# Stick-breaking attention: sums over later key blocks formed on GpSimd ahead of the products with ones

## The reference

```python
z = einsum('bhqd,bhkd->bhqk', q_b, k) * scale
log_beta = log_sigmoid(z)
log_1m = where(strict, log_sigmoid(-z), 0.0)              # strict: key < query
acc = cumsum(log_1m, axis=3, reverse=True) - log_1m       # over the later keys
w = where(strict, exp(log_beta + acc), 0.0)
out = einsum('bhqk,bhkd->bhqd', w, v)
```

## Time and profile before

| | |
|---|---|
| median of the runs | 1338.36 us (1338.24 to 1340.0, 3 runs) |
| the profiled execution | span 1338.4 us, next to nothing around it |
| TensorE products | busy 1297.8 us, 97% of the span |
| TensorE weight loads | 1092.2 us, 82% (beside the products) |
| VectorE | 734.4 us, 55% |
| ScalarE | 554.5 us, 41% |
| GpSimd | 260.2 us, 19% |
| granted clock of TensorE | mean 0.990 of full |

### The profile page before, as it was taken

How to read it: one execution, slowest core, us unless ns; L and a number is a source line. 1 busy time by engine, 2 the same in 40 slices (tenths; PEclk the granted TensorE clock), 3 DMA queues, 4 the chain that set the end, 5 groups by cost and what they waited for, 6 DMA issues and landing times.

```text
span 1338.4 us, 17696 instructions
## 1 busy us (share of the span) xinstructions
PE 1297.8 (97%) x6599; PEld 1092.2 (82%) x6599; DVE 734.4 (55%) x998; ACT 554.5 (41%) x885; POOL 260.2 (19%) x205
## 2 busy tenths in 40 slices
PE   6979999999999999999999999999999999999997
PEld 5667788898888888888898888887988888887885
DVE  4777655538645445422288788686575544553223
ACT  4466666546322332222364555464453222322112
POOL 0532200025211111000051111321431111110002
PEclk8999999999999999999999999999999999999999
DMA  4412222122333333333222111311223333332331
GB/s 158 128 49 64 72 72 71 48 79 80 110 97 101 101 94 92 89 98 94 84 75 68 48 48 55 87 48 48 80 86 104 94 94 98 100 115 79 95 95 63
DMA packets 190503, 112.34 MB, mean 84 GB/s; under 512 B 13696, under 2 KB 184773, under 8 KB 190446
## 3 DMA queue, kind: packets, MB, share of 16 engines
q1 hardware_dynamic: 188636, 106.81, 27.5%
q0 software_dynamic: 640, 2.10, 0.6%
q10 hardware_dynamic: 1170, 2.66, 0.5%
HBM read 109.43 MB, written 4.74 MB: 85 GB/s over the span
## 4 chain that ended last, share of the span: by engine, by line
PE 85%; DVE 8%; ACT 3%; issue 2%; POOL 1%; DMA 0%; POOLq 0%; ACTq 0%; SPq 0%; DVEq 0%
PE banks L432 26%; PE banks L434 25%; PE banks L433 25%; PE banks L1711 3%; DVE w_lo L427 1%; PE banks L1741 1%; PE banks L1629 1%; PE banks L1458 1%; DVE logits L1420 1%; PE banks L481 1%; DVE tf L701 1%; ACT logits L1431 1%; DVE probsT_lo L1470 1%; POOL stick_lo L1728 0%; DVE u_lo L711 0%
## 5 line engine op out<-in xcount | busy, mean ns | idle before, releaser
L427 DVE TENSOR_TENSOR w_lo<-w_raw,w_hi 128x1024 fp32r<-128x1024 f32 (+3 forms) x200 | 288.2, 1444 | 270.7 <-ACT w_hi L420 270.4
L432 PE MATMUL banks<-u_hi,w_hi 128*128 128x512 f32 (+1 forms) x1112 | 425.5, 383 | 5.8 <-DVE w_lo L427 4.3
L434 PE MATMUL banks<-u_hi,w_lo 128*128 128x512 f32 (+1 forms) x1112 | 419.5, 377 | 0.0
L433 PE MATMUL banks<-u_lo,w_hi 128*128 128x512 f32 (+1 forms) x1112 | 419.2, 377 | 0.0
L420 ACT ACTIVATE w_hi<-w_raw 128x1024 fp32r<-128x1024 f32 (+3 forms) x200 | 206.1, 1031 | 282.6 <-PE banks L434 282.5
L432 PEld LDWEIGHTS banks<-u_hi,w_hi 128*128 128x128 f32 x1112 | 210.6, 189 | 45.8 <-issue 4.9
L434 PEld LDWEIGHTS banks<-u_hi,w_lo 128*128 128x128 f32 x1112 | 210.3, 189 | 38.9
L433 PEld LDWEIGHTS banks<-u_lo,w_hi 128*128 128x128 f32 x1112 | 210.5, 189 | 38.0 <-issue 1.0
L904 POOL TENSOR_TENSOR up<-up,gate 128x512 f32<-128x512 f32 x44 | 71.9, 1635 | 375.1 <-DVE up L930 358.3
L885 ACT ACTIVATE gate<-gate 128x512 f32<-128x512 f32 x44 | 27.8, 632 | 202.2 <-DVE gate L926 202.2
L1728 POOL TENSOR_TENSOR stick_lo<-softplus,stick_hi 128x1280 fp32r<-128x1280 f32 x14 | 44.1, 3162 | 157.0 <-DVE stick_hi L1724 157.0
(11 more groups left out here) (256 smaller groups left out, 1983.1 us busy)
## 6 DMA issues: line engine op xcount, KB each, us to landing
w_raw<-in_ffn_w_gate_up_dram SPq DMA_DIRECT2D x88, 512.0 KB, 3.7
w_raw<-in_ffn_w_down_dram SPq DMA_DIRECT2D x30, 512.0 KB, 3.6
w_raw<-in_sb_w_qkv_dram SPq DMA_DIRECT2D x24, 512.0 KB, 3.8
w_raw<-in_ab_w_in_dram SPq DMA_DIRECT2D x17, 512.0 KB, 3.7
w_raw<-in_ffn_w_down_dram SPq DMA_DIRECT2D x16, 448.0 KB, 3.6
w_raw<-in_ab_w_out_dram SPq DMA_DIRECT2D x8, 512.0 KB, 3.9
w_raw<-in_sb_w_out_dram SPq DMA_DIRECT2D x8, 512.0 KB, 4.7
bias_by_distance<-bias_rows ACTq DMA_DIRECT2D x1, 2560.0 KB
```

The costliest lines, as they stand in the source:

```text
L427: dve.tensor_tensor(wl[:, c.slot, 0:w], raw[:, c.slot, 0:w], wh[:, c.slot, 0:w].bitcast(F32), ALU.subtract).then_inc(w_lo, 1)
L432: nc.tensor.matmul(o, lh, rh, start=start, stop=False, skip_group_check=True)
L433: nc.tensor.matmul(o, lh, rl, start=False, stop=False, skip_group_check=True)
L434: return nc.tensor.matmul(o, ll, rh, start=False, stop=stop, skip_group_check=True)
```

## The change

In `c_pe` the three blocks of later keys that block 0 has, and the two that block 1 has, are no longer multiplied one by one. Their softplus is added up first: `later` holds, in 384 columns, the sum of blocks 1, 2 and 3 and, in 256 columns (from `LATER0`), the sum of blocks 2 and 3, each where its queries have them. Per head:

- ScalarE copies two pieces of 128 columns (`later_act`);
- GpSimd adds 128 columns, and then 384 (`later_pool`);
- ScalarE rounds all 640 columns to the hi part (`later_hi`), GpSimd subtracts for the lo part (`later_lo`); both go into `stick_hi` and `stick_lo`, which are free at that time;
- TensorE does the four triangle blocks and the one product with ones of block 2 as before, then waits for `ls_lo`, then multiplies the two sums with ones: 14 products instead of 20.

The steps are put into the written-out orders; on GpSimd both heads' steps stand ahead of `stick_lo`. The buffer `later` (640 columns) makes the stage's space larger by 96 columns a partition, and `tri_f` moves into the place of `sq_sum`.

```diff
+LATER0, LATER1, LATER = T - P, T - 2 * P, 2 * T - 3 * P
...
+            later = sb(s, "later_keys", [P, LATER])
-
-        sb(ctx, "stage_buffers", [P, 27680])
+        sb(ctx, "stage_buffers", [P, 27776])
...
-        tri_f = sb(ctx, "tri_f", [P, P])
...
+        with ExitStack() as s:
+            tri_f = sb(s, "tri_f", [P, P])
...
+        def later_act(act, p, e):
+            hh = p * 2 + e
+            act.wait_ge(ns_f, hh + 1)
+            if not (isinstance(p, int) and p == 0 and e == 0):
+                act.wait_ge(ls_lo, hh)
+            act.activation(later[:, 0:P], lsp[:, e, COL_AT[1]:COL_AT[1] + P], ACT.Copy)
+            act.activation(later[:, LATER0:LATER0 + P], lsp[:, e, COL_AT[2]:COL_AT[2] + P], ACT.Copy)\
+                .then_inc(ls_copied, 1)
+
+        def later_pool(pool, p, e):
+            hh = p * 2 + e
+            pool.wait_ge(ns_f, hh + 1)
+            if not (isinstance(p, int) and p == 0 and e == 0):
+                pool.wait_ge(ls_lo, hh)
+            nc.gpsimd.tensor_tensor(later[:, LATER0 + P:LATER], lsp[:, e, COL_AT[2] + P:COL_AT[2] + 2 * P],
+                                    lsp[:, e, COL_AT[3]:COL_AT[3] + P], ALU.add).then_inc(ls_one, 1)
+            pool.wait_ge(ls_copied, hh + 1)
+            pool.wait_ge(ls_one, hh + 1)
+            nc.gpsimd.tensor_tensor(later[:, P:LATER0], lsp[:, e, COL_AT[1] + P:COL_AT[1] + 3 * P],
+                                    later[:, LATER0:LATER], ALU.add).then_inc(ls_all, 1)
+
+        def later_hi(act, p, e):
+            hh = p * 2 + e
+            act.wait_ge(ls_all, hh + 1)
+            if not (isinstance(p, int) and p == 0):
+                act.wait_ge(sv_done, 2 * p - 1 + e)
+            act.activation(swh[:, e, 0:LATER], later[:, :], ACT.Copy).then_inc(ls_hi, 1)
+
+        def later_lo(eng, op, p, e):
+            eng.wait_ge(ls_hi, p * 2 + e + 1)
+            op(swl[:, e, 0:LATER], later[:, :], swh[:, e, 0:LATER].bitcast(F32), ALU.subtract).then_inc(ls_lo, 1)
+
         def c_pe(pe, p, e):
             hh = p * 2 + e
             pe.wait_ge(ns_lo, hh + 1)
-            Z = ZB[e]
+            def add(lt, at, parts, src, w):
+                for n in parts:
+                    mm = nc.tensor.matmul(ZB[e][:, at:at + w], lt[:, :], n[:, e, src:src + w],
+                                          start=False, stop=False, skip_group_check=True)
+                return mm
             for j in range(TT):
-                for jj in range(j, TT):
-                    at, w = COL_AT[j] + (jj - j) * P, T - P * jj
-                    lt = negtri if jj == j else negones
-                    for n in (nsh, nsl):
-                        mm = nc.tensor.matmul(Z[:, at:at + w], lt[:, :], n[:, e, COL_AT[jj]:COL_AT[jj] + w],
-                                              start=False, stop=False, skip_group_check=True)
-            mm.then_inc(c_done, 1)
+                add(negtri, COL_AT[j], (nsh, nsl), COL_AT[j], T - P * j)
+            add(negones, COL_AT[2] + P, (nsh, nsl), COL_AT[3], P)
+            pe.wait_ge(ls_lo, hh + 1)
+            add(negones, COL_AT[0] + P, (swh, swl), 0, T - P)
+            add(negones, COL_AT[1] + P, (swh, swl), LATER0, T - 2 * P).then_inc(c_done, 1)
...
             z_act_ln(act, p, 1)
+            if not last and not first:
+                split_hi(act, sb_chunk(p + 2, 0))
+            later_act(act, p, 0)
             if not last:
                 if not first:
-                    split_hi(act, sb_chunk(p + 2, 0))
                     sb_k_act(act, p + 1, q)
+                later_hi(act, p, 0)
                 split_hi(act, sb_chunk(p + 2, 1))
+            else:
+                later_hi(act, p, 0)
             if not (first or last):
                 sb_o_act(act, p - 1, 1, O_BANK)
+            later_act(act, p, 1)
+            later_hi(act, p, 1)
             if not last:
                 split_hi(act, sb_chunk(p + 2, 2))
             w_act(act, p, 0)
...
         def sb_pair_pool(pool, p, par, first=False, q_next=True, last=False):
+            for e in range(2):
+                later_pool(pool, p, e)
+                later_lo(pool, nc.gpsimd.tensor_tensor, p, e)
             if not last:
                 for e in range(2):
                     stick_lo(pool, nc.gpsimd.tensor_tensor, p, e)
```

More of the change, by code:

```diff
@@ L365, in bass_hybrid_two_layers @@
         ns_f, ns_hi, ns_lo = sem("softplus_ready"), sem("softplus_hi"), sem("softplus_lo")
+        ls_copied, ls_one, ls_all = sem("later_copied"), sem("later_third_added"), sem("later_second_added")
+        ls_hi, ls_lo = sem("later_hi"), sem("later_lo")
         c_done, w_exp, sw_hi, sw_lo = sem("stick_sums"), sem("stick_exp"), sem("stick_hi"), sem("stick_lo")
```

## The result

The changed kernel takes 1350.72 us (median of 4 executions, 1350.03 to 1352.82) against 1339.07 in the same comparison (1338.24 to 1340.0): ratio 1.0088, interval 1.0076 to 1.01, so 0.9% slower, 11.7 us. The forecast was 1360, slower, with a range of 1341 to 1367. Direction and range held; the size was 9 us too high. The profiled execution has a span of 1348.1 us and a granted clock of 0.987.

The account below looks back on a forecast made before the run. TensorE, never idle in the middle windows, was taken as the bound. 1338.4 + 4.8 (first pair) + 2.5 (its clock fall) + 5.4 (pairs 1 to 5) + 3.4 (their clock) + 5.2 (pairs 6, 7) = 1359.7, so 1360; range 1341 to 1367.

Parts of the forecast that it names:

- The turns of GpSimd and VectorE: Stick-breaking stage: the two engines shut each other out and alternate whole instructions, making sb_scale 2.2 us late in a middle pair.
- a middle pair: Pairs 1 to 5: TensorE's transposes start at 809.4, not 808.33, +1.07 us each, +5.4 for five.
- GpSimd yields: Rival, chance 0.14: VectorE's next instruction goes ahead of waiting GpSimd, sb_scale is not late, middle pairs save 1.16 each; 1342.
- the walk: One middle pair followed in time, engine by engine, from softplus to transposes; it gave +1.07 us a pair.
- The six products: Per head on TensorE: 14 products instead of 20 save 0.67 us, 10.7 us over 16 heads.
- The rival in which the products alone decide: Rival "Faster", chance 0.06: ls_lo arrives within 1.5 us of the start of a head's sums everywhere; -10.7 us, 1328.
- The first pair: Pair 0: head 0's sums wait 6.1 us behind head 1's logarithm; +4.8 us, plus 2.5 for a clock fall.
- The clock in the middle: Pairs 1 to 5: waits of 1.9 us bring two falls of the granted clock, 3.4 us, bounds 0 and 8.5.
- The rival with a fall in every pair: Rival, chance 0.14: the clock falls in every pair, adding 3 x 1.7 in pairs 1 to 5 and 1.7 in the last; 1366.5.
- Pairs 6 and 7: End of the stage: VectorE's delay reaches stick_lo and head 1's softplus; +5.2 us with pair 6's own loss, bounds +2.2 and +7.
- the carried lateness: Pairs 6 and 7: VectorE's 2.2 us delay passes through stick_lo, so head 1's softplus comes at 910.5, not 908.3.

Follow-up runs that it names:

- the kernel with 16 columns: Changed kernel with GpSimd's three new instructions a head 16 columns wide instead of 128, 384 and 640, sums not formed: 1328.89 us, ratio 0.9927.
- the order: Changed kernel with VectorE running sb_scale first behind nsp_lo of head 1, then the weight split, then sb_o_dve: 1338.39 us, ratio 0.9999.

## Why the prediction was right, and where it was off

**The turns of GpSimd and VectorE** were the right mechanism, and the pair went as walked: `nsp_lo` 1.90, `sb_k_lo` 0.95 and `sb_o_dve` 1.95 instead of 1.49, 0.68 and 0.69; a wait of 1.6 to 1.7 us before the transposes (forecast 1.9); a middle pair +0.94 us (forecast +1.07). The rival "GpSimd yields" (1342) falls with the 1.95. That the length of GpSimd's instructions makes the loss, and not the extra waits or ScalarE's work, is shown by the kernel with 16 columns; that an instruction of VectorE that reads PSUM is spared, by the order: `sb_scale` 0.69 beside GpSimd's 640 columns. `sb_scale` has only one input in SBUF, and no run separates that from its reading PSUM. (The Trainium skill, GPSIMD Engine Reference, Key points, names VectorE instructions with two SBUF inputs or in a two-port mode as those that contend with GpSimd; the traces agree, with 1.95 for `sb_o_dve`, which has two, and 0.69 for `sb_scale`.)

**One width was wrong.** The description of the change and the walk gave GpSimd's second sum 384 columns and 1.02 us; the code and the trace have 256, and 0.72 us where nothing was in its way. The other 128 of the 384 are ScalarE's copy. The other prices held: 0.46 for 128 columns, 1.53 to 1.57 for 640, 0.74 for ScalarE's rounding, 0.29 to 0.31 for its copies (forecast 0.33). It accounts for part of the 0.13 us by which the pair was overestimated; how much, no run separates.

**The six products** are worth 0.62 us a head. The forecast took 0.67, with 0.11 for a product of 128 columns; the steps in the earlier trace rows, 0.24 for two of 256 and twice 0.17 for two of 128, give 0.58. (The Trainium skill's rule in TensorE: Matmul & The Clock Gate, section "Wait — 56ns, not 53.3ns?", gave 0.44; the measured 0.62 decides.) That VectorE would stop TensorE 1.16 us further on was nearly right: it came at 0.98. The rival in which the products alone decide (1328) fails twice: `ls_lo` is 5.8 us late in the first head, and even without any sum the saving stops at 0.98 a pair.

**The first pair**: a wait of 5.83 (forecast 6.1) and a clock of 0.52 over 6 us, 2.9 us lost (forecast 2.5). The step is +6.3 against +7.3; the wait is 0.3 us shorter, and GpSimd's narrower sum, 0.3 us less, is in its chain. The rest of the difference no run separates.

**The clock in the middle** was taken too dearly. Of the five waits of 1.6 to 1.7 us in pairs 1 to 5 one brought a fall, the one in pair 5 (0.72 over 6 us, 1.7 us), not two; the sixth, in pair 6, brought none. That is 1.7 us of what the forecast had too much in the stage. Which of the waits bring a fall the runs don't settle: with the first head's sums earlier the same six waits brought two, in pairs 4 and 6. The rival with a fall in every pair (1366.5) is out. Pair 7 in turn was to keep its one fall and got two: windows of the kernel after, behind the waits of 2.06 and of 1.50 and 1.27 us.

```profile
912.00:918.00 6.00, 4.16 (x11) 3.29 (x12) 5.84 (x6) 3.41 (x6) 2.83 (x3) 0.72 0.00 1
922.00:928.00 6.00, 4.73 (x20) 4.06 (x19) 4.11 (x4) 3.10 (x3) 1.64 (x2) 0.73 0.00 0
```

**Pairs 6 and 7** were +5.2 in the forecast. The step behind pair 6's transposes is +4.7 with the second fall in it, but pair 6's own 0.7 (2.4 less the 1.7 of the clock) lies ahead of it: +5.4 in all. Less the 1.6 us of that fall it is 3.8, so the carried lateness was smaller than walked, and a fall that was not foreseen made up for it. That the sum came near there is luck.

**The term that was missing** is the places of the buffers. The prediction named neither the 96 columns nor `tri_f` and thus gave them nothing. Alone they are worth 6 us. Stage 21.3 forecast against 17.7 measured, 3.6 us, and 6.1 us outside it make 9.7, against the 9.3 us between 1360 and 1350.72; the forecast started from 1338.4, and the median of the comparison was 1339.07. Without that gain the change would have been about 1.3% slower, not 0.9 (an estimate, 17.7 us in 1339).

## What to carry to other kernels

Work given to an idle GpSimd is not free if VectorE is near its limit: each of its instructions can hold VectorE up for as long as it runs, unless what VectorE runs beside it reads PSUM. Here 5.5 us of new work on GpSimd in a pair (twice 0.46, 0.72 and 1.55) made VectorE 1.94 us later. Then the order decides: put the PSUM reader on which TensorE waits at that place, and let the block fall on something nobody stands for; here that took 12 us off the changed kernel, and leaving out the first and last pairs, where nothing hides the new chain, another 10, to 10.6 us below the kernel before, somewhat over half of which the moved buffers give. And when an edit changes the size of a buffer, run that size alone with no work changed, or its effect is booked to the change.

## What the hardware did that was not expected

Products of 512 columns on `hidden` start every 0.235 us in the kernel before and every 0.227 in the same kernel with its buffers moved by 96 columns; a shift of 32 columns does the same, and one of 64 nothing. The timeline of TensorE in the kernel before (six steps in 1.41 us):

```profile
599.66 0.40 PE L433 MATMUL banks<-hidden_lo,w_hi 128*128 128x512 f32 x1
...
601.07 0.40 PE L433 MATMUL banks<-hidden_lo,w_hi 128*128 128x512 f32 x1
```

and with 27776 columns (six steps in 1.36 us):

```profile
599.63 0.39 PE L433 MATMUL banks<-hidden_hi,w_hi 128*128 128x512 f32 x1
...
600.99 0.39 PE L433 MATMUL banks<-hidden_hi,w_hi 128*128 128x512 f32 x1
```

The clock fell behind one of six waits of 1.6 to 1.7 us in the kernel after, the one in pair 5. In the kernel with the first head's sums earlier it fell behind two of them, in pairs 4 and 6 (0.72 over 840 to 846 and over 898 to 904), waits of 1.68 and 1.60 us. What sets these apart is open.
